# Dilated attention: value products with 64 stationary columns, both heads of a pair in one bank

## The reference, cut to what matters

```python
    s = jnp.einsum('nhqd,nhkd->nhqk', qb, kb).astype(jnp.float32) * scale
    s = jnp.where(band & (start - front + ki >= 0), s, -jnp.inf)
    m = jnp.max(s, axis=-1, keepdims=True)
    p = jnp.exp(s - m)
    den = jnp.sum(p, axis=-1, keepdims=True)
    o = jnp.einsum('nhqk,nhkd->nhqd', (p / den).astype(vb.dtype), vb)
    return o, (m + jnp.log(den))[..., 0]
...
w = jax.nn.softmax(jnp.stack(lses, axis=0), axis=0)
o = jnp.sum(w[..., None] * jnp.stack(outs, axis=0), axis=0)
```

## Time and profile before

| what | value |
|---|---|
| median of 3 runs | 4246.82 us (4241.04 to 4247.91) |
| the profiled execution, its own time | 4245.55 us |
| its span | 4243.8 us |
| TensorE busy | 95% of the span |
| VectorE / ScalarE / GpSimd busy | 62% / 38% / 13% |
| the two attention stages of the change | 646 to 750 us and 972 to 1080 us |

### The profile page before, as it was taken

How to read it: one execution, slowest core, us unless ns; L and a number is a source line. 1 busy time by engine, 2 the same in 40 slices (tenths; PEclk the granted TensorE clock), 3 DMA queues, 4 the chain that set the end, 5 groups by cost and what they waited for, 6 DMA issues and landing times. The chain is left out here.

```text
span 4243.8 us, 54933 instructions
## 1 busy us (share of the span) xinstructions
PE 4012.8 (95%) x19521; PEld 3372.3 (79%) x19521; DVE 2635.1 (62%) x4865; ACT 1622.5 (38%) x2364; POOL 534.0 (13%) x549
## 2 busy tenths in 40 slices
PE   7999998998999989999899999999999999999998
PEld 6887776776788878887677888757889999988886
DVE  6632766576465256524773332585998788688887
ACT  3222235335322133223683221453335555533333
POOL 1100000000010001000100000000004455233332
PEclk9999999999999989999899999989999999999999
DMA  7632320320364226523002222202338989899997
GB/s 280 228 119 94 115 84 6 114 79 31 141 232 158 99 95 230 189 95 108 6 1 97 92 99 99 88 4 98 125 115 285 341 324 350 310 337 353 354 353 277
DMA packets 140165, 700.59 MB, mean 165 GB/s; under 512 B 18375, under 2 KB 19750, under 8 KB 94638
## 3 DMA queue, kind: packets, MB, share of 16 engines
q1 hardware_dynamic: 66574, 423.83, 27.9%
q0 software_dynamic: 73440, 274.76, 17.6%
HBM read 635.55 MB, written 59.80 MB: 164 GB/s over the span
## 5 line engine op out<-in xcount | busy, mean ns | idle before, releaser
L112 DVE TENSOR_TENSOR w_lo<-raw,w_hi 128x2048 fp32r<-128x2048 f32 x331 | 758.6, 2292 | 711.4 <-ACT w_hi L104 707.0
L124 PE MATMUL ps<-x_hi,w_hi 128*128 128x512 f32 (+1 forms) x2896 | 1092.5, 377 | 60.0 <-DVE w_lo L112 36.1
L125 PE MATMUL ps<-x_lo,w_hi 128*128 128x512 f32 (+1 forms) x2896 | 1078.2, 372 | 0.0
L126 PE MATMUL ps<-x_hi,w_lo 128*128 128x512 f32 (+1 forms) x2896 | 1077.8, 372 | 0.0
L104 ACT ACTIVATE w_hi<-raw 128x2048 fp32r<-128x2048 f32 x331 | 632.6, 1911 | 666.8 <-PE ps L126 422.1
L124 PEld LDWEIGHTS ps<-x_hi,w_hi 128*128 128x128 f32 x2896 | 549.0, 190 | 148.0 <-issue 54.7
L126 PEld LDWEIGHTS ps<-x_hi,w_lo 128*128 128x128 f32 x2896 | 548.0, 189 | 75.3
L125 PEld LDWEIGHTS ps<-x_lo,w_hi 128*128 128x128 f32 x2896 | 549.2, 190 | 73.2
L2340 POOL DMA_INDIRECT ph_rows<-in_peer_u,ph_names x128 | 222.2, 1736 | 1281.2 <-DVE ph_names L2710 1017.4
L2423 PE MATMUL ps<-w_hi,px_gh 128*128 128x512 f32 x768 | 300.2, 391 | 4.7 <-DVE px_gl L2763 4.7
L2423 PE MATMUL ps<-w_lo,px_gh 128*128 128x512 f32 x768 | 300.0, 391 | 0.0
(11 more groups left out here) (404 smaller groups left out, 5637.5 us busy)
## 6 DMA issues: line engine op xcount, KB each, us to landing
raw<-in_slabs SPq DMA_DIRECT2D x331, 1024.0 KB, 4.9
ada_ring<-in_w_ada POOLq DMA_DIRECT2D x160, 512.0 KB, 5.3
act_dram<-px_act SPq DMA_DIRECT2D x64, 384.0 KB, 7.4
gate_dram<-ps_g SPq DMA_DIRECT2D x12, 2048.0 KB, 12.7
px_g<-gate_dram POOLq DMA_DIRECT2D x32, 768.0 KB, 8.2
px_ai<-act_dram POOLq DMA_DIRECT2D x64, 384.0 KB, 6.5
h_dram<-h SPq DMA_DIRECT2D x2, 2048.0 KB, 8.0
h<-h_dram SPq DMA_DIRECT2D x2, 2048.0 KB, 8.4
```

Of the source, the lines that this page charges most:

```text
L112: nc.vector.tensor_tensor(k.wlo[:, c % 2, :], k.raw[:, c % 2, :], k.whi[:, c % 2, :].bitcast(F32), ALU.subtract).then_inc(k.raw_free, 1)
L124: mm(out, hi, rhs_hi, start=start, stop=False)
L125: mm(out, hi, rhs_lo, start=False, stop=False)
L126: return mm(out, lo, rhs_hi, start=False, stop=stop)
```

## The change

The value products take only the head's own 64 columns of `vt` as stationary operand, and write only that head's 64 rows. Both heads of a pair so share one bank, and the pairs use banks 6 and 7 in turn. The two heads' matmuls alternate within each group and block. `values` of a unit waits once, for the copies of both heads (`copied` at 6u + 6), where before head 0's products waited for head 0's copies alone. `high` and `low` run once for a pair, on 128 rows; the wait for `o` asks only that the pair before the last has been read. `low` moves behind both `scaled` on VectorE.

```diff
-            def values(u, h2):
+            def out(p, h2):
+                return k.ps[rows(h2), (6 + p % 2) * T:(7 + p % 2) * T]
+
+            def values(u):
                 p, rq = divmod(u, NB)
-                v = 2 * u + h2
-                pe.wait_ge(s["copied"], 3 * v + 3)
-                if rq == 0 and p:
-                    pe.wait_ge(s["o"], 2 * p - 1 + h2)
+                pe.wait_ge(s["copied"], 6 * u + 6)
+                if rq == 0 and p > 1:
+                    pe.wait_ge(s["o"], p - 1)
                 for g in (1, 2):
-                    last = nc.tensor.matmul(bank(k, 6 + h2, P, rq * P), vt[:, g, rq, p * P:(p + 1) * P],
-                                            pt1[:, u % 2, h2, (g - 1) * P:g * P], start=rq == 0 and g == 1, stop=False)
-                last.then_inc(s["pv"], 1)
+                    for h2 in range(2):
+                        last = nc.tensor.matmul(out(p, h2)[:, rq * P:(rq + 1) * P],
+                                                vt[:, g, rq, p * P + HD * h2:p * P + HD * (h2 + 1)],
+                                                pt1[:, u % 2, h2, (g - 1) * P:g * P], start=rq == 0 and g == 1, stop=False)
+                        if g == 2:
+                            last.then_inc(s["pv"], 1)
-            def values0(p, h2):
-                out = bank(k, 6 + h2).rearrange("p (r m) -> p r m", r=NB)
+            def values0(p):
                 for i in range(NB):
                     at = min(32 * i, HD)
-                    last = nc.tensor.matmul(out[:, :, at:at + HD], vt[:, 0, i, p * P:(p + 1) * P],
-                                            pt0[:, h2, i, :, :], start=False, stop=i == NB - 1)
-                last.then_inc(s["pv0"], 1)
+                    for h2 in range(2):
+                        last = nc.tensor.matmul(out(p, h2).rearrange("p (r m) -> p r m", r=NB)[:, :, at:at + HD],
+                                                vt[:, 0, i, p * P + HD * h2:p * P + HD * (h2 + 1)],
+                                                pt0[:, h2, i, :, :], start=False, stop=i == NB - 1)
+                        if i == NB - 1:
+                            last.then_inc(s["pv0"], 1)
...
-                for h2 in range(2):
-                    values(u, h2)
-                    if u % NB == NB - 1:
-                        values0(u // NB, h2)
+                values(u)
+                if u % NB == NB - 1:
+                    values0(u // NB)
...
-            def high(p, h2):
-                act.wait_ge(s["pv0"], 2 * p + h2 + 1)
-                A(out_hi(p)[rows(h2)], k.ps[rows(h2), (6 + h2) * T:(7 + h2) * T], ACT.Copy).then_inc(s["high"], 1)
+            def high(p):
+                act.wait_ge(s["pv0"], 2 * p + 2)
+                A(out_hi(p), bank(k, 6 + p % 2), ACT.Copy).then_inc(s["high"], 1)
...
-                    if u % NB == 0 and u:
-                        high(u // NB - 1, h2)
+                    if u % NB == 0 and u and h2 == 0:
+                        high(u // NB - 1)
                     copies(u, h2)
...
-            def low(p, h2):
-                ve.wait_ge(s["high"], 2 * p + h2 + 1)
-                V.tensor_tensor(out_lo(p)[rows(h2)], k.ps[rows(h2), (6 + h2) * T:(7 + h2) * T],
-                                out_hi(p)[rows(h2)].bitcast(F32), ALU.subtract).then_inc(s["o"], 1)
+            def low(p):
+                ve.wait_ge(s["high"], p + 1)
+                V.tensor_tensor(out_lo(p), bank(k, 6 + p % 2), out_hi(p).bitcast(F32), ALU.subtract).then_inc(s["o"], 1)
...
                 for h2 in range(2):
-                    if u % NB == 0 and u:
-                        low(u // NB - 1, h2)
                     if u + 1 < U:
                         scaled(u + 1, h2)
-            for h2 in range(2):
-                low(U // NB - 1, h2)
+                if u % NB == 0 and u:
+                    low(u // NB - 1)
+            low(U // NB - 1)
```

More of the change, by code:

```diff
@@ L825, in _ @@
                         exps(u + 1, h2)
-                    if u % NB == 0 and u:
-                        high(u // NB - 1, h2)
+                    if u % NB == 0 and u and h2 == 0:
+                        high(u // NB - 1)
                     copies(u, h2)
-            for h2 in range(2):
-                high(U // NB - 1, h2)
+            high(U // NB - 1)
         @blk.vector
```

## The result

In the first comparison the changed kernel took 4214.89 us (median of 5, 4200.16 to 4219.07) and the kernel before 4246.0 (5, 4238.35 to 4247.91): a ratio of 0.9925, 95% interval 0.9905 to 0.9946. It is faster, by 31 us where 22 were forecast, and the time lies 4 us under the range. Later comparisons on one chip each gave 0.9940 (0.9918 to 0.9963) and 0.9941 (0.9925 to 0.9956). Over all executions, 63 of the kernel before with a mean of 4240.9 us and 17 of the changed one with 4214.9, the change is worth 26.0 us, with a standard error of 1.9.

A forecast was written before the change was run, and what follows sets the result against it. TensorE leads, but the order of waits was taken to bound the kernel. From 4245.55 us, 17.2 (closing, opening, last units) and 4.8 (clock) came off: 4223.6, or 4225 with 1.3 for the median; range 4219 to 4254.

The forecast's parts named there:

- plain unit: Unit without values0 or waits for `low`, 9 a stage: head 1's copies set its end; stays 5.13 us, nothing saved.
- opening unit: Unit where TensorE waits for `low`, 3 a stage: waits go, 6.61 us becomes 5.13, 1.48 saved each.
- A column pair costs what a row pair costs: Value products: two heads' matmuls on different columns run together, 0.11 us a pass pair, 0.22 for values0.
- first rival: Two heads' value products run one after the other: 10.8 us slower, 4257 to 4258, or 4253 without clock drops; chance 0.19.
- The rule on weight loads: Skill's rule against the forecast: loads overlap matmuls in flight only across row groups, so the heads' products would follow each other.
- closing unit: Unit with values0, 3 a stage besides the last: scores start at 675.39 instead of 676.33, 0.94 us saved each.
- last unit, copies' end to the end of values0: End of each stage: head 1's copy ends at 744.86, values0 at 747.35 instead of 748.67; 1.32 us saved.
- VectorE's pause behind an opening unit: VectorE's idle time ahead of the next maxima, with `low` behind both divisions: 0.28 us left, enough but thin.
- clock in the two stages: Three drops to half clock around ends of opening units, 1.59 us each, go with the waits: 4.8 us saved.
- Halving the columns by itself buys nothing: Value products: a pass costs the same 0.11 us with 64 stationary columns, so gain needs both heads running together.
- The clock falls more often: Rival: TensorE's fewer passes and longer idle bring twelve drops at 1.6 us, giving back 19: about 4245, no change; chance 0.07.
- Half an overlap: Rival: second head one pass behind, or VectorE's slack used up; 4 to 12 us less gain, 4229 to 4237; chance 0.08.

The follow-up runs named there:

- e5: Changed kernel with each unit's values and values0 issued one unit later, behind the next scores: 4189.22 us, ratio 0.9885 to the kernel before.
- e3: Changed kernel with all pairs in one bank (always bank 6), so first values wait for `low` of the pair before: 4236.17 us, 0.9985 of the kernel before.
- e4: Changed kernel with 105 unused identity transposes ahead of each of the two stages' first scores: 4230.05 us, ratio 0.9972 to the kernel before.
- e6: Changed kernel with both heads' products on the same 64 columns and output rows: 4241.66 us, ratio 1.0001 to the kernel before.
- e2: Changed kernel with all of head 0's value products, then all of head 1's, not in turn: 4217.92 us, ratio 0.9947 to the kernel before.

## Why the prediction was wrong, and where it was right

**What bounds the kernel.** Right for the plain unit (e5) and for the opening unit (e3). One clause of it was wrong in its use: "nothing else moves". The rest of the program moves from one execution to the next, from 4019 to 4032 us in the five profiles of the two kernels, and e4 shows that it can depend on what stands in the two stages. That the change itself moves it is neither shown nor excluded. The five runs of the changed kernel in the first comparison spread over 19 us, where the three of before that I had spread over 7.

**A column pair costs what a row pair costs.** Right. I took 0.11 and 0.22 us a pass from the value rows of before, and from the score rows that a pair costs no more; measured are (0.66 - 0.27) / 3 = 0.13, with a first step from idle in it, and (1.90 - 0.38) / 7 = 0.217. e6 gives the other bounds, 1.09 and 3.62 us, and with them the time of the first rival: 4242 us against the 4253 to 4258 that I gave it. Its unit costs were right: over the changed kernel 0.42 us in a plain unit and 2.16 in a closing one, where I had 0.44 and 2.17. Its level was too high, in the main by the two errors below, the level of the kernel before and the clock.

**The rule on weight loads.** The Trainium skill, "TensorE: Matmul & The Clock Gate", Part 3, says that a load overlaps with matmuls in flight only where the row group differs. This case's traces do not agree: all 128 rows are shared, and the loads of the two heads, x8 in 0.42 us, run beside matmuls in flight. In the kernel before, too, the load at 668.003 us (0.189 long) lies within the record of the matmul before it on the same tile (from 667.897, 0.377 long). That loads overlap is thus nothing that the change adds. The same part's figure of the Trainium skill for column tiles points the right way. The measurement decides.

**The terms of the sum.**

| term | forecast | measured |
|---|---|---|
| plain unit | 5.13, no change | 5.08 |
| closing unit | 6.85 | 6.80 |
| opening unit | 5.13 | 5.08 |
| last unit, copies' end to the end of values0 | 744.86 to 747.35: 2.49 | 733.66 to 736.10: 2.44 |
| VectorE's pause behind an opening unit | 0.28 | 0.37 |
| all without the clock | 17.2 | 23.1 - 4.8 = 18.3 |
| clock in the two stages | 4.8 | 4.8 in the profile used; 8.8 in the second |
| level of the kernel before | 4246.8 (3 executions) | 4240.9 (mean of 63) |

The 0.05 us in each unit were not forecast: scores start 0.59 us after values instead of 0.64, since the first step from idle is 0.16 us and not 0.21. "Halving the columns by itself buys nothing" was wrong by that much. Up to the last scores of both stages this makes 1.4 us; the end of each stage then gained 1.14 us where 1.32 were forecast. The terms without the clock are right to 1.1 us.

**The step that failed is the clock's term and its bound, and with it the level that the sum starts from.** The clock first. I took 4.8 us saved, said that it "is bounded by 4.8 saved", and had that from one execution. A second execution of the kernel before had stretches at 0.5 behind five opening units instead of three (one of them 6.8 us long), and its two stages together are 4.0 us longer than in the first; so its loss there is about 4.8 + 4.0 = 8.8 us. The direction was right: with the wait gone the stretches behind opening units go, in all three profiles, where the kernel before has eight behind twelve such units. With 18.3 and 4.8 to 8.8 the change gives 23 to 27 us, and 26.0 is the mean over all executions.

The level was the larger error. The changed kernel takes 4214.9 us, 10 under the 4225 forecast. Of these 10, 4 are the gain (26.0 for 22.0) and 6 are the start of the sum, the median of three executions (4246.8) where 63 have a mean of 4240.9. All three medians of the changed kernel, 4214.9, 4214.2 and 4214.3, lie under the range.

The other 5 us of the first comparison's 31 were most likely chance. Its five executions of the kernel before had a mean of 4244.0 us against 4240.9 over all, and its five of the changed kernel 4212.2 against 4214.9; the difference of such means has a standard error of 3.8. My range of 4219 to 4254 took its lower end from the parts of the sum alone, 6 us under the forecast, and had no room for a wrong level.

**Rivals.** One after the other: refuted, and its price confirmed by e6. The clock falls more often: refuted; it falls less. (The argument against it named only the first stage, whose first units kept 1.0; those of the second had the 6.8 us at 0.5.) Half an overlap: refuted in this order of the products, and real in another (e2, 7.5 us in the stages). That the wait for `low` would only move: refuted by 0.37 us left on VectorE.

## What to carry to other kernels

In this kernel two matmuls that use different halves of the array's columns and write different rows of the output run at the same time, and it is this, not the smaller operand, that pays (27 us between e6 and the change); put them in turn, since at four in a row the overlap was partly lost (e2). Free banks and overlap are both needed: without the second bank 20 of the 26 us are gone (e3, by the means), and without the overlap all of them (e6). Before counting what a shorter engine gives, look at which wait ends last in each kind of unit: here the 18 plain units of 32 gained almost nothing until their values were issued behind the next scores. A clock term read from one execution is one draw, and so is a level read from three: ask for a second profile and more executions before bounding either, and give the range the spread of the whole program.

## What the runs showed of the hardware

- Column pairs in 32-bit floats overlap fully: 16 passes over 256 moving columns, eight of each head, in 1.90 us, against 3.62 on the same columns.
- TensorE starts matmuls of another column half ahead of their turn, past two matmuls of 32-bit floats (four passes) in e2: with two a head the order makes no difference (0.66 us both ways), with four it is 2.81 us instead of 1.90.
- With 64 stationary columns a weight load takes 0.137 us, with 128 it takes 0.192; the time of a pass does not change (0.11 us for 128 moving columns).
- The clock stood at 1.0 through 105 transposes back to back (11.52 us busy in 11.6) in both stages of e4. Behind them TensorE was busy for 1.83 us of 3.8 in the first stage and for 1.84 in the second; in the first the clock then fell to 0.5, at 658.5, in the second it did not. Why is open.
- A subtraction or copy from PSUM costs the same on 128 rows as on 64 (0.68 and 0.60 us against 0.68 and 0.59).
